# Six pairs of 1024-wide projections computed as seven block products each, ahead of the state-space branch

## The chip, the cores and the metric

One core of one Trainium2 chip runs the whole program: two transformer blocks on 1024 tokens of width 1024, in float32. The metric is the device time of one execution in microseconds (us), as the median of several runs; lower is better.

## What is computed

The change touches only the first block. With `x` of 1024 tokens by 1024 features it computes (cut to what matters):

```
xn   = rmsnorm(x, attn_norm_g)
proj = xn @ w_in                      # 38 feature tiles of 128: 0-3 pool, 4-9 / 10-15 / 16-21 q / k / v of
                                      # dilated attention, 22-33 q, k, v of stick-breaking, 34-37 state space
y_pool, y_dil, y_sb, y_s5 = the four branches of proj
for b, yb in enumerate((y_pool, y_dil, y_sb, y_s5)):
    merged += sigmoid(xn @ w_gate[b]) * (yb @ w_branch[b])   # w_gate: 4 x 8 feature tiles of 128
x = x + merged @ w_out                # then a gated FFN, then the second block
```

The second block is modulated by `cond @ w_ada`, a vector-matrix product whose 48 tiles of 512 KB are read and reduced while the first block is still running ("conditioning").

## The kernel before

**Layout and products.** Activations are kept transposed, features on partitions. A *product* (`product`, `product_steps`) is one output tile of 128 features by 1024 tokens: for each of 8 input tiles of 128 features, three float32r matmuls (high part of weight and input, then each low part with the other's high part) for each half of 512 tokens, 48 matmuls of 128x128 by 512. One input tile (6 matmuls) is a *step*. The normalised input is held as `XH[0]` (high part, `xhi`) and `XH[1]` (low part, `xlo`). A product with 4 input tiles (`w_br3`, `w_br0`, `w_glu`) has 24 matmuls.

**Weights.** `weight_plan` lists every product in the order in which TensorE takes them (`PLAN`). A ring of three buffers serves them: SyncE loads unit i+5 into `raw` (`load_weights`), ScalarE rounds unit i+2 to `whi` (`weights_hi`, L436), VectorE subtracts to `wlo` (`weights_lo`, L441). `begin_sp`, `begin_act` and `begin_dve` are called at unit i on each engine; `weights_hi` of unit j must wait until the product of unit j-3 is over, because it shares that buffer. No scheduler orders anything: each engine runs its own hand-written sequence and waits on counters.

**Order in the first block.** `input_*` normalises x and computes `w_in` tiles 34 and 35; `s5_*` is the state-space branch. Its own matmuls are small, so 13 products (`BESIDE`: `w_in` 36, 37 and eleven gates in `EARLY_S5`) are cut into steps and put between its stages by the table `SLOTS` (21 steps beside the making of `CL`, 3 and 10 beside the kernel rows, and so on). Early gates leave for DRAM (`spill`) and come back in their merge. `merge_*(3)` then multiplies gates and branch products, `pool_*`, `merge_*(0)`, `dil_*` (dilated attention, three groups g), `merge_*(1)`, `sb_*`, `merge_*(2)` follow. In a merge, turn ft computes gate ft+1 (only if it isn't early; 48 matmuls) and branch product ft (24 matmuls in merges 3 and 0). Beside merges 3, 0 and 1, conditioning (`cond_*`) takes 3 steps per turn, one before the branch product and two after: a step is one 512 KB load into a ring of three `adr` buffers on SyncE and one multiply-add into `ada` on VectorE (L1244, L1247); after 8 of them TensorE turns `ada` into 8 columns (L1271), from which VectorE makes `mod`.

**Dilated attention** starts each group with products for k and v (in group 0 also q), each copied out of PSUM by ScalarE (`K`, `Vf`, L1712), then transposes v (`turned`), and then interleaves scores, softmax and outputs of 8 blocks with the steps of the next group's q products.

**Seven products.** The two FFN up-projections already compute a pair of 1024-deep products as seven block products instead of eight (`seven_pe`, L2517). Two weight tiles by two halves of the inputs make a 2x2 block matrix, and tokens are cut in halves too; with sums of weight blocks (on GpSimd, L2480 to L2489) and of input blocks (made once), seven products of 4 input tiles by 512 tokens, 12 matmuls each, are enough, and additions on VectorE and GpSimd (`P1`, `U2`, `U3`, `P5`; tile name `prt`) make the four results.

Of the kernel before, what the change touches and what calls it, by code (L numbers as in the profile page):

```python
# [8 lines left out]
F32 = mybir.dt.float32  # L9
# [5 lines left out]
T = 1024  # L15
# [67 lines left out]
EARLY_S5 = ((3, 2), (3, 4), (3, 6), (0, 0), (0, 2), (0, 4), (0, 6), (1, 0), (1, 6), (2, 6), (3, 0))  # L83
# [4 lines left out]
EARLY = EARLY_S5 + EARLY_DIL + EARLY_SB  # L88
# [12 lines left out]
def weight_plan():  # L101
# [22 lines left out]
    tiles("w_in", range(34, 38), 8)  # L124
    tiles("w_gate", [8 * b + ft for b, ft in EARLY_S5], 8)
# [4 lines left out]
    tiles("w_in", [4, 5], 8)  # L130
    for g in range(3):
        tiles("w_in", [10 + 2 * g, 11 + 2 * g, 16 + 2 * g, 17 + 2 * g] + ([6 + 2 * g, 7 + 2 * g] if g < 2 else []), 8)
# [46 lines left out]
def used_part(i):  # L179
# [26 lines left out]
    "sums_dve": "x_add sq_add t1_sum sum1 t2_sum t_sum2",  # L206
# [160 lines left out]
def build(nc, A, out, scr, spill, bsc, hid):  # L367
    from contextlib import ExitStack
    ctx = ExitStack()
    with ctx:  # L370
# [228 lines left out]
        def input_act(act):  # L599
# [13 lines left out]
            def high(k, hf):  # L613
                act.wait_ge("xn_g", k, hf)
                hi_of(act, XH[0][:, k, half[hf]], xtmp[k % 3][:, half[hf]], "xn_hi", k, hf)
# [18 lines left out]
        def input_dve(dve):  # L634
# [6 lines left out]
            def low(k, hf):  # L641
                dve.wait_ge("xn_hi", k, hf)
                lo_of(dve, XH[1][:, k, half[hf]], xtmp[k % 3][:, half[hf]], XH[0][:, k, half[hf]], "xn_lo", k, hf)

            for hf in range(2):
                dve.wait_ge("xn_rstd", hf)
                for k in range(8):
                    if k >= 3:
                        dve.wait_ge("xn_lo", k - 3, hf)
                    dve.e.scalar_tensor_tensor(xtmp[k % 3][:, half[hf]], X[:, k, half[hf]], vec("attn_g", k), xrstd[:, half[hf]], ALU.mult, ALU.mult).then_inc(*give("xn_g", k, hf))  # L650
# [9 lines left out]
            weights_lo(dve, 2)  # L660
            for g in range(3):
# [4 lines left out]
            next(powers, None)  # L666
            begin_dve(dve, "w_in", 34)
            begin_dve(dve, "w_in", 35)
            s5_coefficients(dve)

        XNH = [(XH[0][:, k, :], XH[1][:, k, :], (("xn_lo", k, 0), ("xn_lo", k, 1))) for k in range(8)]
        XN = [(hi, lo, ready[1]) for hi, lo, ready in XNH]
# [15 lines left out]
        q1 = mem("q1", u_at - 1280, [128, 4, 16])  # L688
        q2 = mem("q2", u_at - 1024, [128, 16, 16])
# [26 lines left out]
        def s5_powers(dve):  # L716
# [47 lines left out]
            for _ in range(2):  # L764
                tt(t1, si, si, ALU.mult)
                stt(si, si, 2.0, co, ALU.mult, ALU.mult)
                ts(co, t1, -2.0, 1.0, ALU.mult, ALU.add)
            tt(nr, mag, co, ALU.mult)
# [16 lines left out]
        def s5_coefficients(dve):  # L785
# [15 lines left out]

            for _ in range(3):
# [4 lines left out]

            b3 = lambda x: x.unsqueeze(2).to_broadcast([128, 16, 16])
# [29 lines left out]

        BESIDE = [("w_in", 36), ("w_in", 37)] + [("w_gate", 8 * b + ft) for b, ft in EARLY_S5]
        BESIDE0 = PLAN.index(("w_in", 36, 0, 8))  # L840
        SLOTS = [("cl", 21), ("k", 3), ("ks", 10)]
# [3874 lines left out]
```

## Time and profile before

| | us |
|---|---|
| median of 3 runs | 3344.96 |
| lowest, highest | 3342.58, 3346.75 |
| the profiled execution, own time | 3346.08 |
| its span in the trace | 3344.40 |

TensorE is busy in 3267.9 of the 3344.4 us. The trace gives for each instruction its start, its length, the idle time before it on its engine and the instruction that ended that idle time. The length of a matmul in the trace includes its way through the array and overlaps the next one; the pace of TensorE is read from the distance of starts. Two matmuls of the same form are merged into one row ("x2").

### The profile page before, as it was taken

The numbers are of one execution on the slowest core, as the hardware profiler recorded it, in microseconds if no ns is written. First come the engines' busy times: TensorE is split into PE (matmuls) and PEld (weight loads), VectorE is DVE, ScalarE is ACT, GpSimd is POOL, SyncE is SP. The second block draws the span as 40 slices with busy tenths as digits, with TensorE's granted clock in tenths as the row PEclk, the third lists the DMA queues.
The fourth block names the chain that finished last, engine by engine and source line by source line (L and its number), as shares of the span: only waits on it lengthen the run. The fifth ranks groups of instructions, "written<-read, shape, count | busy, mean of one in ns | idle before, by whom it ended". The sixth has DMA issues, their size and how long they took to land.

```text
span 3344.4 us, 38691 instructions
## 1 busy us (share of the span) xinstructions
PE 3267.9 (98%) x15672; PEld 2676.9 (80%) x15672; DVE 1955.6 (58%) x2362; ACT 1317.5 (39%) x1888; POOL 467.6 (14%) x369
## 2 busy tenths in 40 slices
PE   8999999999999999999999999999989999999998
PEld 6888888877877778888888887777788778888886
DVE  8564462333756534677773265445476788888226
ACT  4342211444256523433331147343555554444213
POOL 0000000000000000445540020000020025554000
PEclk9999999999999999999999999999999999999999
DMA  3313242112520123233238323121204322234721
GB/s 125 78 57 132 92 162 72 46 51 68 193 70 27 62 85 131 88 112 114 101 113 334 130 85 114 62 99 44 102 1 170 114 88 109 105 114 164 304 98 51
DMA packets 116402, 356.91 MB, mean 107 GB/s; under 512 B 16232, under 2 KB 26216, under 8 KB 116208
## 3 DMA queue, kind: packets, MB, share of 16 engines
q1 hardware_dynamic: 114112, 354.10, 30.6%
q8 instruction: 124, 2.03, 0.3%
q10 hardware_dynamic: 2112, 0.33, 0.1%
q14 instruction: 54, 0.44, 0.0%
HBM read 267.63 MB, written 85.58 MB: 106 GB/s over the span
## 4 chain that ended last, share of the span: by engine, by line
PE 86%; DVE 6%; ACT 5%; issue 1%; DMA 1%; ACTq 0%; SPq 0%; DVEq 0%
PE PS L496 45%; PE PS L2517 22%; PE PS L479 8%; PE PS L1980 1%; PE PS L514 1%; PE PS L1633 1%; ACT whi L436 1%; ACT dS L1689 1%; PE PS L3961 1%; DVE wlo L441 0%; DVE FT L3834 0%; PE PS L3972 0%; PE PS L1608 0%; DVE GS L3490 0%; DVE dO L1754 0%
## 5 line engine op out<-in xcount | busy, mean ns | idle before, releaser
L441 DVE TENSOR_TENSOR wlo<-raw,whi 128x1024 fp32r<-128x1024 f32 (+3 forms) x380 | 482.5, 1270 | 389.5 <-ACT whi L436 386.7
L436 ACT CAST whi<-raw 128x1024 fp32r<-128x1024 f32 (+3 forms) x380 | 359.1, 945 | 690.2 <-PE PS L496 339.8
L496 PE MATMUL PS<-xhi,whi 128*128 128x512 f32 x1872 | 600.3, 402 | 7.3 <-DVE wlo L441 2.8
L496 PE MATMUL PS<-xlo,whi 128*128 128x512 f32 x1872 | 578.1, 390 | 0.0
L496 PE MATMUL PS<-xhi,wlo 128*128 128x512 f32 x1872 | 577.1, 389 | 0.0
L496 PEld LDWEIGHTS PS<-xhi,whi 128*128 128x128 f32 x1872 | 344.3, 188 | 91.8 <-issue 15.4
L496 PEld LDWEIGHTS PS<-xlo,whi 128*128 128x128 f32 x1872 | 351.4, 188 | 75.2
L496 PEld LDWEIGHTS PS<-xhi,wlo 128*128 128x128 f32 x1872 | 351.4, 188 | 74.8
L2517 PE MATMUL PS<-tf,whi 128*128 128x512 f32 x936 | 288.0, 389 | 0.0
L2517 PE MATMUL PS<-xhi,whi 128*128 128x512 f32 x624 | 243.5, 390 | 2.5 <-DVE xlo L2502 2.5
L2517 PE MATMUL PS<-xlo,whi 128*128 128x512 f32 x624 | 243.2, 390 | 0.0
L2517 PE MATMUL PS<-xhi,wlo 128*128 128x512 f32 x624 | 243.2, 390 | 0.0
L2517 PEld LDWEIGHTS PS<-tf,whi 128*128 128x128 f32 x936 | 175.7, 188 | 36.4
L2517 PE MATMUL PS<-tf,wlo 128*128 128x512 f32 x468 | 182.1, 389 | 0.0
L2116 POOL TENSOR_SCALAR_AFFINE_SELECT sbt<-sbt 128x128 f32<-128x128 f32 x64 | 17.8, 293 | 1072.8 <-DVE sbt L2137 1041.8
L2517 PEld LDWEIGHTS PS<-xhi,whi 128*128 128x128 f32 x624 | 117.5, 188 | 27.2 <-DVE xlo L2502 3.0
L2480 POOL TENSOR_TENSOR raw<-raw 128x512 f32<-128x512 f32 x39 | 76.0, 1948 | 438.3 <-DVE wlo L441 328.6
L2517 PEld LDWEIGHTS PS<-xlo,whi 128*128 128x128 f32 x624 | 117.6, 188 | 24.4
L2517 PEld LDWEIGHTS PS<-xhi,wlo 128*128 128x128 f32 x624 | 117.4, 188 | 24.5
L479 PE MATMUL PS<-xhi,whi 128*128 128x512 f32 x256 | 109.7, 429 | 6.3 <-DVE xlo L530 5.3
L496 PE MATMUL PS<-yhi,whi 128*128 128x512 f32 x352 | 109.1, 391 | 1.1 <-ACT gearly L888 1.1
L479 PE MATMUL PS<-slot,whi 128*128 128x512 f32 x352 | 110.1, 394 | 0.0
(613 smaller groups left out, 5482.4 us busy)
## 6 DMA issues: line engine op xcount, KB each, us to landing
raw<-in_w_up SPq DMA_DIRECT2D x88, 512.0 KB, 4.0
hid<-hs SPq DMA_DIRECT2D x88, 512.0 KB, 3.6
raw<-in_w_in SPq DMA_DIRECT2D x67, 512.0 KB, 3.5
slot<-hid SPq DMA_DIRECT2D x56, 512.0 KB, 6.8
adr<-in_w_ada SPq DMA_DIRECT2D x48, 512.0 KB, 4.8
raw<-in_w_down SPq DMA_DIRECT2D x40, 512.0 KB, 3.6
raw<-in_w_gate SPq DMA_DIRECT2D x32, 512.0 KB, 3.5
merged<-hid SPq DMA_DIRECT2D x16, 512.0 KB, 12.4
```

The source lines that it names most:

```text
L436: act.e.copy(whis[place(i)][:, ks, :], raws[i % RING][:, ks, :]).then_inc(*give("w_hi", i))
L441: dve.e.tensor_tensor(wlos[place(i)][:, ks, :], raws[i % RING][:, ks, :], whis[place(i)][:, ks, :].bitcast(F32), ALU.subtract).then_inc(*g ...
L479: ins = pe.e.matmul(ps[:, half[hf]], w[s][:, k, :], x[:, half[hf]], start=(at == 0 and n == 0), stop=(at == kt - 1 and n == 2))
L496: ins = pe.e.matmul(ps[:, h * 512:(h + 1) * 512], w[s][:, k, :], x[:, h * 512:(h + 1) * 512], start=(at == 0 and n == 0), stop=(at == kt - ...
L514: ins = pe.e.transpose(ps[:, j * 128:(j + 1) * 128], src[:, j * 128:(j + 1) * 128], ident)
L1633: ins = pe.e.matmul(ps[:, 64 * h:64 * h + 64], dP[u % 2][:, n, k, :], Vt[:, k0 // 128 + k, 64 * h:64 * h + 64], start=(k == 0), stop=(k == ...
L1689: act.e.activation(S[:, h, 256 - W:256], S[:, h, 256 - W:256], ACT.Exp, bias=st[:, h:h + 1], accum_out=O[:, 260 + h:261 + h]).then_inc(*gi ...
L1980: pe.e.matmul(ob[:, cs], sbVt[:, kb, :], sbwk[n % 4][0][:, cs], start=u["first"], stop=(kb == 0), skip_group_check=True).then_inc(*give("s ...
L2116: pool.e.affine_select(out=t[:, ds], in_=t[:, ds], pattern=[[1, 128]], compare_op=ALU.is_gt, fill=0.0, base=0, channel_multiplier=-1).then ...
L2480: pool.e.tensor_tensor(s[:, 0:4, :], b[:, 0:4, :], b[:, 4:8, :], ALU.add).then_inc(*pool.step())
L2517: ins = pe.e.matmul(ps, ws[w][:, at + k, :], xs[:, k, :], start=(k == 0 and n == 0), stop=(k == 3 and n == 2))
L3961: ins = pe.e.matmul(ps[:, sl[n]], Me[:, sl[n]], odd[:, sl[n]], start=True, stop=True)
```

## The change

1. `PASS` names six pairs: gates (3,3) and (3,7), gates (0,3) and (0,7), `w_in` 4 and 5 (q of group 0), and `w_in` 16/17, 18/19, 20/21 (v of the three groups). They are taken out of the merges and of dilated attention and computed by a new stage between `w_in` 37 and the state-space work, each pair as seven block products (`pass_pe`). Their 12 results go to DRAM (`pass_store`) and are read back where they are used.
2. The input sums `PT` are made in place in `X` by VectorE (`pass_sum`), split by `pass_hi` and `pass_lo`; one of them overwrites tiles 0 to 3, second half, of `XH`, which is saved to DRAM before (`xn_saved`) and loaded back after the last use (`xn_back`). To free that use early, the last pair computes its p5 first. The first product after the stage takes input tiles 4 to 7 first.
3. `w_in` 36 and 37 run ahead of the stage; the small operations for the state-space coefficients (`s5_powers`, `s5_coefficients`) are cut in pieces and run between VectorE's work for pairs 1 to 4. The state-space stage has 12 gates beside it (2,5 is new); its first slots are 9, 5 and 12 steps.
4. In merges 3 and 0 conditioning takes 4 + 2 steps in a turn that has a gate product and 2 + 0 in a turn that has none.
5. Group 0 of dilated attention starts with k instead of q, and all groups have no v product; q and v are loaded from DRAM.

```diff
+PASS = ((("w_gate", 27), ("w_gate", 31)), (("w_gate", 3), ("w_gate", 7)), (("w_in", 4), ("w_in", 5)),
+        (("w_in", 16), ("w_in", 17)), (("w_in", 18), ("w_in", 19)), (("w_in", 20), ("w_in", 21)))
...
+        def pass_pe(pe):
...
+                if p == NPASS - 1:
+                    part(s12, 0, PTF[1], "p5", ("sv_p5", 0, p), "sv_5", 0, p)
+                part(a, 0, PX11, "p1", ("sv_p1", 0, p), "sv_1", 0, p)
+                part(a, 4, PX21, "p2", ("sv_c11", 0, p), "prod", a)
+                pe.wait_ge("t_lo", 0, 4)
+                part(b, 4, PTF[4], "p4", ("sv_c21", 0, p), "prod", b)
+                pe.wait_ge("t_lo", 0, 1)
+                if p < NPASS - 1:
+                    part(s12, 0, PTF[1], "p5", ("sv_p5", 0, p), "sv_5", 0, p)
+                pe.wait_ge("t_lo", 0, 2)
+                part(s12, 4, PTF[2], "p6", ("sv_u2", 0, p), "prod", s12)
+                part(s34, 0, PTF[3], "p7", ("sv_u3", 0, p), "sv_7", 0, p)
+                part(s34, 4, PX22, "p3", ("sv_c12", 0, p), "prod", s34)
...
+        def pass_act(act):
+            for p in range(NPASS):
+                begin_act(act, *PASS[p][0])
+                if p == 0:
+                    pass_hi(act, 1)
+                    pass_hi(act, 2)
+                else:
+                    act.wait_ge("sv_c12", 0, p - 1)
...
+        def pass_dve(dve, others):
...
+                begin_dve(dve, *PASS[p][1])
+                if p:
+                    next(beside, None)
+                begin_dve(dve, "pass_s12", p)
+                dve.wait_ge("prod", i + 2)
...
+        def pass_sp(sp):
...
+                begin_sp(sp, "pass_s34", p)
+            sp.wait_ge("sv_5", 0, NPASS - 1)
+            for m in range(2):
+                sp.e.dma_start(PTF[1][m].bitcast(F32), BACKUP[m]).then_inc(*land("xn_back", m))
...
-        SLOTS = [("cl", 21), ("k", 3), ("ks", 10)]
+        SLOTS = [("cl", 9), ("k", 5), ("ks", 12)]
...
+        def beside_steps(b, ft):
+
+            if b not in (3, 0):
+                return 1, 2
+            return (2, 0) if (b, ft + 1) in EARLY or ft == 7 else (4, 2)
...
-                for n, ring in enumerate((side_ring, o_ring)):
-                    product(pe, ring, "w_in", 16 + 2 * g + n, XN, ("dil_v", g, n))
                 turned(g, 0)
```

Three places show what the change moves. The first is VectorE in merge 3, turns 0 to 3 (`merged` is the multiply with the branch product, `ada` a conditioning step, `mod` the wait for TensorE's 8 columns). Before:

```order
L1348 TENSOR_TENSOR merged_79<-PS,gearly_135 128x1024 [waits gate,prod]
L1244 TENSOR_SCALAR ada_141<-adr_138,cond_52 128x1024 [waits cond,adr0]
...
L1348 TENSOR_TENSOR merged_79<-PS,sgl_136 128x1024 [waits gate,prod]
...
L1348 TENSOR_TENSOR merged_79<-PS,sgl_137 128x1024 [waits gate_in0,prod]
L1247 SCALAR_TENSOR_TENSOR ada_141<-adr_138,cond_52,ada_141 128x1024 [waits ada,adr0]
L1247 SCALAR_TENSOR_TENSOR ada_141<-adr_139,cond_52,ada_141 128x1024 [waits ada,adr1]
L441 TENSOR_TENSOR wlo_62<-raw_56,whi_59 128x512 [waits w_hi]
L1348 TENSOR_TENSOR merged_79<-PS,sgl_136 128x1024 [waits gate,prod]
L1258 TENSOR_TENSOR mod_51<-PS,V_49 128x8 [waits pe_sums]
```

Now:

```order
L1603 TENSOR_TENSOR merged_79<-PS,gearly_135 128x1024 [waits gate,prod]
L1493 SCALAR_TENSOR_TENSOR ada_154<-adr_151,cond_52,ada_154 128x1024 [waits ada,adr0]
L1493 SCALAR_TENSOR_TENSOR ada_154<-adr_152,cond_52,ada_154 128x1024 [waits ada,adr1]
L1493 SCALAR_TENSOR_TENSOR ada_154<-adr_153,cond_52,ada_154 128x1024 [waits ada,adr2]
L1493 SCALAR_TENSOR_TENSOR ada_154<-adr_151,cond_52,ada_154 128x1024 [waits ada,adr0]
L446 TENSOR_TENSOR wlo_63<-raw_57,whi_60 128x512 [waits w_hi]
L1603 TENSOR_TENSOR merged_79<-PS,sgl_136 128x1024 [waits gate,prod]
L1493 SCALAR_TENSOR_TENSOR ada_154<-adr_152,cond_52,ada_154 128x1024 [waits ada,adr1]
L446 TENSOR_TENSOR wlo_64<-raw_58,whi_61 128x1024 [waits w_hi]
L1603 TENSOR_TENSOR merged_79<-PS,sgl_137 128x1024 [waits gate_in0,prod]
L1504 TENSOR_TENSOR mod_51<-PS,V_49 128x8 [waits pe_sums]
```

The eighth `ada` step stood after the third `merged`, with the fourth `merged` and its turn behind it before TensorE's columns; now it stands after the second `merged`, and TensorE's columns come right ahead of the fourth branch product.

The second place is ScalarE at the start of group 1 of dilated attention (`K` and `Vf` are the copies of k and v out of PSUM). Before:

```order
L436 CAST whi_61<-raw_58 128x1024 [waits w_raw2]
L1712 COPY K_119_167<-PS 128x256x4 [waits prod]
L436 CAST whi_59<-raw_56 128x1024 [waits w_raw0]
L1712 COPY Vf_168<-PS 128x256x4 [waits prod]
L436 CAST whi_60<-raw_57 128x1024 [waits w_raw1]
L1712 COPY Vf_168<-PS 128x256x4 [waits prod]
L1689 ACTIVATE dS_173,dO_179<-dS_173,dstat_178 128x128 [waits dil_st00,dil_dve]
```

Now:

```order
L441 CAST whi_60<-raw_57 128x1024 [waits w_raw1]
L1978 COPY K_132_180<-PS 128x256x4 [waits prod]
L441 CAST whi_61<-raw_58 128x1024 [waits w_raw2]
L1957 ACTIVATE dS_186,dO_192<-dS_186,dstat_191 128x128 [waits dil_st00,dil_dve]
```

Between the last copy of k and the first exponential of the scores two v products with their copies are gone.

The third place is SyncE at the last pair of the new stage (`put` is a result on its way out, `xhi` and `xlo` from `spill` are the input tiles that come back). Nothing like it was there before. Now:

```order
L1050 DMA spill<-put_148 128x1024
L434 DMA raw_58<-in_w_gate 128x1024 [waits w_lo]
L1063 DMA xhi_75<-spill 128x4x512 [waits seven_pe]
L1063 DMA xlo_76<-spill 128x4x512
L1050 DMA spill<-put_149 128x1024 [waits seven_dve]
```

The two loads that bring the input tiles back stand behind a weight load with a wait of its own.

## Rows read from the trace of the kernel before

**Rows 1.** The page: busy time, share of the span, instructions of TensorE.
```profile
PE 3267.9 (98%) x15672; PEld 2676.9 (80%) x15672; DVE 1955.6 (58%) x2362; ACT 1317.5 (39%) x1888; POOL 467.6 (14%) x369
```

**Rows 2.** Waits of TensorE, 50 to 290 us: total, times, longest.
```profile
PE PS L940 <- DVE CL L1105: 1.5, 2, 1.3
PE PS L514 <- ACT work L1041: 1.4, 1, 1.4
PE PS L496 <- DVE wlo L441: 1.3, 1, 1.3
```

**Rows 3.** Timeline of TensorE, two FFN pairs: start, length (us), operation, idle before.
```profile
1484.63 0.61 PE L2517 MATMUL PS<-tf,whi 128*128 128x512 f32 x2
...
1503.67 0.61 PE L2517 MATMUL PS<-tf,whi 128*128 128x512 f32 x2
```

**Rows 4.** Timeline of VectorE, 47 to 62 us.
```profile
51.65 3.60 DVE L700 TENSOR_SCALAR w<-w 128x16 f32<-128x16 f32 x1
...
61.53 1.22 DVE L441 TENSOR_TENSOR wlo<-raw,whi 128x1024 fp32r<-128x1024 f32 x1
```

**Rows 5.** Timeline of GpSimd, 0 to 110 us.
```profile
51.69 3.53 POOL L925 MEMSET Mk<- 128x4096 f32 x1 [51.17 <-DMA bsc<-brow]
```

**Rows 6.** Timeline of TensorE around the start of `w_in` 37.
```profile
61.01 0.61 PE L496 MATMUL PS<-xhi,wlo 128*128 128x512 f32 x2
62.89 0.70 PE L496 MATMUL PS<-xhi,whi 128*128 128x512 f32 x2 [1.27 <-DVE wlo L441]
```

**Rows 7.** The FFN's input sums: min/median/max ns, starts; and TensorE's wait for them.
```profile
L2498 ACT CAST tf<-merged x4: 1901/1906/1912, 1356.9 to 2707.3; 128x2048 fp32r<-128x2048 f32 x4
...
L2502 DVE TENSOR_TENSOR tf<-merged,tf x4: 2275/2284/3376, 1362.5 to 2709.2; 128x2048 fp32r<-128x2048 f32 x4
...
PE PS L2517 <- DVE xlo L2502: 2.5, 1, 2.5
```

**Rows 8.** Timelines of ScalarE, VectorE and GpSimd in the same FFN pairs.
```profile
1484.88 1.06 ACT L436 CAST whi<-raw 128x1024 fp32r<-128x1024 f32 x1 [1.17 <-PE PS L2517]
...
1498.43 0.69 DVE L2579 TENSOR_TENSOR fsg<-PS,prt 128x512 f32<-128x512 f32 x1 [1.30 <-PE PS L2517]
1499.15 2.21 DVE L2738 TENSOR_TENSOR fsg<-fsg,rstd 128x1024 f32<-128x1024 f32 x1
...
1498.98 1.30 POOL L2489 TENSOR_TENSOR raw<-raw,raw 128x512 f32<-128x512 f32 x1
```

**Rows 9.** Timeline of VectorE: first and last of six operations for half of `CL`.
```profile
73.65 1.35 DVE L704 TENSOR_TENSOR CL<-PR,BC 128x1152 f32<-128x1152 f32 x1
...
80.61 1.36 DVE L1105 SCALAR_TENSOR_TENSOR CL<-CL,cltmp 128x1152 f32<-128x1152 f32 x1
```

**Rows 10.** DMA, 0 to 20 us: rate in 40 slices of 0.5 us; one issue's size and landing.
```profile
GB/s 0 0 0 47 185 366 336 135 160 279 287 283 324 287 320 320 332 369 410 434 434 410 401 410 406 401 402 406 402 381 389 381 385 389 422 410 406 420 415 382
...
x<-in_xT SPq DMA_DIRECT2D x16, 256.0 KB, 7.0
```

**Rows 11.** Copies of k (min/median/max ns), and TensorE where group 0's transposes start.
```profile
L1712 ACT COPY K<-PS x6: 1014/1995/2017, 552.8 to 758.6; 128x1024 f32<-128x1024 f32 x6
...
585.26 1.03 PE L514 MATMUL PS<-ident,Vf 128*128 128x128 f32 x8
586.23 0.71 PE L1608 MATMUL PS<-K,Qs 64*128 64x128 f32 x8
```

**Rows 12.** VectorE in merge 0, a conditioning step's length, and the landing of its loads.
```profile
467.50 1.22 DVE L1350 TENSOR_TENSOR sg<-PS,sg 128x1024 f32<-128x1024 f32 x1 [2.22 <-PE PS L496]
...
469.90 2.67 DVE L1247 SCALAR_TENSOR_TENSOR ada<-adr,cond,ada 128x1024 f32<-128x1024 f32 x2
...
L1247 DVE SCALAR_TENSOR_TENSOR ada<-adr,cond,ada x28: 1273/1283/1289, 306.4 to 504.6; 128x1024 f32<-128x1024 f32 x28
...
DMA to landing us min/median/max: 3.7/4.8/7.0
```

**Rows 13.** Merge 3: length, then busy us and instructions of PE, PEld, DVE, ACT, POOL, clock, DMA share, GB/s.
```profile
290.00:376.50 86.50, 86.50 (x391) 71.91 (x390) 42.69 (x41) 16.06 (x20) 0.00 (x0) 1.00 0.51 172
```

More of the change, by code:

```diff
@@ L863, in stream @@
                 for p, (name, ft) in enumerate(BESIDE):
-                    done = ("s5_u", ft - 34) if name == "w_in" else ("gate", ft // 8, ft % 8)
-                    yield from product_steps(pe, [0, 1] if p % 2 == 0 else [1, 0], name, ft, XN, done)
+                    order = (4, 5, 6, 7, 0, 1, 2, 3) if p == 0 else None
+                    yield from product_steps(pe, [0, 1] if p % 2 == 0 else [1, 0], name, ft, XN, ("gate", ft // 8, ft % 8), order=order)
             steps = stream()
@@ L909, in s5_sp @@
             begin_sp(sp, "w_in", 35)
+            sp.wait_ge("xn_lo", 3, 1)
+            for m in range(2):
+                sp.e.dma_start(BACKUP[m], PTF[1][m].bitcast(F32)).then_inc(*land("xn_saved", m))
+            begin_sp(sp, "w_in", 36)
+            begin_sp(sp, "w_in", 37)
+            pass_sp(sp)
             beside_sp(sp, "cl")
@@ L928, in s5_pe @@
             rows_ring = [2, 3]
+            for n in range(2):
+                product(pe, [n], "w_in", 36 + n, XN0, ("s5_u", 2 + n))
+            pass_pe(pe)
             beside = beside_pe(pe)
@@ L1341, in merge_dve @@
                     branch(dve)
-                next(beside, None)
+                for _ in range(beside_steps(b, ft)[0]):
+                    next(beside, None)
                 i = begin_dve(dve, f"w_br{b}", ft)
@@ L1355, in merge_dve @@
                     dve.e.tensor_tensor(merged[:, ft, :], merged[:, ft, :], g, ALU.add).then_inc(*give("merged", b, ft))
-                next(beside, None)
-                next(beside, None)
+                for _ in range(beside_steps(b, ft)[1]):
+                    next(beside, None)
                 if done:
@@ L1381, in merge_sp @@
                     branch(sp)
-                next(beside, None)
+                for _ in range(beside_steps(b, ft)[0]):
+                    next(beside, None)
                 begin_sp(sp, f"w_br{b}", ft)
-                next(beside, None)
-                next(beside, None)
+                for _ in range(beside_steps(b, ft)[1]):
+                    next(beside, None)
             for _ in beside:
```

279 lines of the change are left out of this document (231 added, 48 removed).

## The prediction, made before the changed kernel ran

> **What bounds the kernel now.** I read the page's busy times first: TensorE is busy for 3267.9 of 3344.4 us [rows 1], so only fewer TensorE cycles or fewer TensorE waits can save time, and a new wait of TensorE costs its full length. Next the waits of TensorE where the new stage goes: they are small and single, 1.5 us for `CL`, 1.4 us for `work`, 1.3 us for a `wlo` [rows 2]. Then the pace, from the one place where seven-product pairs already run: the same part of two consecutive FFN pairs starts at 1484.63 and 1503.67 us, so 84 matmuls take 19.04 us, 0.2267 us each, with no idle time noted on any row between [rows 3]. The reader should see that a pair, once running, costs exactly its matmuls: VectorE, ScalarE and GpSimd keep up. What has to be found is what happens at the stage's two ends, and in the three stages that lose products.
>
> **The matmuls.** A pair as two products has 2 x 48 = 96, as seven block products 7 x 12 = 84. Six pairs save 72 x 0.2267 = **16.3 us**. The compiled sequences agree: TensorE has 72 matmuls fewer and no other form changes its count. The new stage adds per pair 5 additions on VectorE, 6 on GpSimd, 2 copies on ScalarE and two more weight splits. FFN pairs carry all of these and more, so in the steady part I cost them at nothing; the cover is VectorE's slack, about 11 of 19 us per pair (4 splits and 5 additions are some 8 us). The small coefficient operations that are put into pairs 1 to 4 take at most about 8 us in one piece, so they fit; if they didn't, TensorE would wait at the next pair's p1.
>
> **What is removed before the stage.** `w_in` 37 starts at 62.89 where its predecessor's pace ends at 61.01 + 2 x 0.2267 = 61.46: 1.43 us [rows 6]. The cause is on VectorE: the `wlo` runs at 61.53, behind a chain of 16-element operations one of which takes 3.60 us instead of 0.17 [rows 4], exactly while GpSimd's memset of `Mk` runs [rows 5]. Both move away; the split then stands behind two sums of 2.3 us and is over near 56 us. Gain **1.4 us**. The other new work here (four sums, two splits by ScalarE and VectorE, the 2 MB save to DRAM) has until p1, 4 or p5 need it, from 72 us on, and by the same lengths it is ready by 69 us.
>
> **The first pair.** One input sum overwrites tiles that `w_in` 37 reads, so its chain starts only when that product ends: copy of U 1.0, weight rounding 1.05, `pass_hi` 1.9, `pass_lo` 2.28, `pass_hi` 1.9, `pass_lo` 2.28 [rows 7, 8] with 0.3 for the first signal: 10.7 us. TensorE has p1, p2, p4, p5 to do, 4 x 2.72 = 10.9. It just fits; the FFN's similar start costs 2.5 us [rows 7]. I take 0.3, between 0 and 2.5.
>
> **The last pair.** Its p5 comes first. p5's weights lie in the buffer that the previous pair's p3 is still reading, so their rounding can't start before that ends: 0.25 us after TensorE's pace passes on (1484.63 and 1484.88) [rows 3, 8], 1.06 of rounding, then VectorE 1.15. But at a pair's boundary GpSimd still has its two weight differences: at 1498.98 for 1.30 us, 0.75 to 2.05 us after the boundary at 1498.23 (19.04 us before p1 of the next), and the VectorE operation with two inputs from SBUF that meets it takes 2.21 instead of 1.22 us [rows 8]. So the split starts at 2.05 and TensorE at **3.3 us**; without that meeting 2.6, with a full one 4. In all other pairs this chain has 8.2 us of cover. The Trainium skill (SBUF — State Buffer, Who interferes with whom) says that a VectorE instruction with two SBUF inputs contends with a GpSimd instruction that reads SBUF and that the loser fully blocks; the trace agrees (2.21 against 1.22 us), and with it the sum has 3.3, without it 2.6.
>
> **The way back.** The tiles that were saved must be back 4 steps after the stage, 24 x 0.2267 = 5.4 us after its end. Although p5 is over early, SyncE reaches these loads only behind a weight load that waits for a split behind p6, 13.6 us into the last pair; with 0.3 signal, 1.05 and 1.2 for the split the issue is at 16.3, and 2.6 MB at the 400 GB/s of the start [rows 10] take 6.5 us. A start-up of 2.4 us comes on top: the fastest 512 KB landing took 3.7 us [rows 12], 1.3 of it data at that rate. That lands at 25.2, where 19.0 + 5.4 = 24.4 is needed. I take **0.8 us**; with the transfers already flowing it is 0, at 250 GB/s it would be 4.8. The page DMA: Bandwidth & Descriptors (Specifications) of the Trainium skill gives about 358 GB/s as the limit of HBM per core; by it the wait would be 1.6 us, but the trace's slices of 400 to 434 speak against it.
>
> **The state-space stage.** Its first slot shrinks from 21 steps to 9, 54 x 0.2267 = 12.2 us. VectorE needs 0.3 + 1.05 + 1.2 for a weight split and 5 x 1.39 + 1.36 = 8.3 for the first half of `CL` [rows 9]: 10.9. So that wait of TensorE (1.5 us) goes too, by a margin of 1.3. The `work` wait (1.4 us) hung on the DMA of `Mk`, which SyncE issued 9 us late, behind an early gate's store; with this gate's store now before it and 2 steps more beside it, it goes. Gain **2.9 us**, with 0 as the other end.
>
> **Merges 3 and 0.** Both lose two gate products, so three turns in a row have only 24 matmuls, 5.44 us. TensorE's 8 columns for the first `ada` now stand ahead of the fourth branch product, 2 x 5.44 = 10.9 us after the first ended (P), behind VectorE's five `ada` steps, one split and one or two `merged`. In merge 0: `merged` 2.7 after P (467.50 to 469.90, with 0.3 from the product's end) [rows 12], `ada` at 1.3 each to 6.6; the next needs a load that could be issued only when a buffer was free, at 4.0, and lands 4.8 later: 8.8, done 10.1; split 0.7, `merged` 2.4, `ada` 1.3: 14.4 with the signal. TensorE waits 3.4; with the shortest landing (3.7) 2.3, with the longest (7.0) 5.6 [rows 12]. In merge 3 each of the two `merged` is one operation of 1.2 us instead of two: the same chain ends 2.3 us earlier, and TensorE waits 1.1 (0 to 3.3). Sum **4.5 us** (2.3 to 8.9).
>
> **Dilated attention.** k's last copy was covered by two v products. Now only 8 transposes, 0.97 us [rows 11], stand between the product and the first scores. The copy starts 0.3 after, takes 1.0 in group 0 and 2.0 in groups 1 and 2 [rows 11], 0.1 signal: waits of 0.4, 1.4 and 1.4, **3.2 us**. The v and q loads (2 MB for group 0) have 21.8 us of cover.
>
> **Sum.** -16.3 - 1.4 - 2.9 + 0.3 + 3.3 + 0.8 + 4.5 + 3.2 = -8.5 us. The profiled execution's own time is 3346.08 (span 3344.40, the rest lies around it and doesn't change); it would become 3337.6. It lies 1.1 above the median of 3344.96, and the median, which I predict, becomes **3336.5**.
>
> **Rivals.** (A) *All new waits hide.* For it: the tables look made to fit, and each margin above is near 1 us. Against it: last pair and copies of k rest on lengths that don't vary. Only those two at their low ends (2.6, 3.0) and 1 us in the merges: 3344.96 - 20.6 + 6.6 = 3331. (B) *The ends and merges run at their high ends*: first pair 2.5, last 4, way back 4.8, merges 8.9, k 3.2 = 23.4, less 16.3, 1.4 and half of 2.9: 3349 if all come at once; with half of the excess 3343. For it: the same loads took up to 7.0 us when several were queued [rows 12]. (C) *Slower: DMA bounds the short turns.* Turns 1 to 3 of each of the two merges move about 9 pieces of 512 KB, 4.7 MB in 16.3 us, 289 GB/s, and VectorE, which waits for the loads in order, also makes the weights. At 170 GB/s they would take 27.7 us, 11.4 more twice: 3336.5 + 22.8 = 3359. It decides from about 200 GB/s down (23.5 us, 7 more each: 3350). Against it: before, three loads, a gate and weights fell into single short turns, and TensorE was busy in all 86.5 us of merge 3 [rows 13]. (D) *The stage doesn't do what it says*: the pairs run at the pace of the other engines, since results are written in other strides here (two of ScalarE's three-way copies take 2.0 instead of 1.0 us [rows 11]). At 1 us per pair 3342.
>
> **Chances.** Forecast (3334 to 3339) 0.46, of which 0.43 is below 3338.3; A 0.17; B and D together 0.30, of which 0.05 is still faster and 0.02 slower; C 0.04; the remaining 0.03 for faults that I don't see, half of it slower. 0.2% is 6.7 us, about what a measurement of this kernel tells from no change: faster is below 3338.3, slower above 3351.7. Faster 0.43 + 0.17 + 0.05 = 0.65, slower 0.02 + 0.04 + 0.01 = 0.07, same 0.28. The range takes A and half of B: 3329 to 3343.5.
>
> **What would show it.** TensorE with 72 fewer matmuls; in the last pair a wait for `wlo` near 3.3 us ahead of p5; a wait for `ada` before the 8 columns, near 1 in merge 3 and 3 in merge 0; three waits for `K`, 0.4, 1.4, 1.4; no wait for `CL` or `work`; the pairs at 19.04 us. The prediction is wrong if pairs are longer than 19.1 us, if the waits for `ada` are absent or above 6 us, or if `xn_back` holds TensorE for more than 4 us.

## The result, and the profile after

The changed kernel takes **3366.4 us** (median of four runs, 3364.0 to 3368.2), the kernel before 3344.9: a ratio of 1.0064 with a 95% interval of 1.0047 to 1.0082. It is slower by 21.5 us where I had forecast 3336.5. One of the eleven runs of experiment 7 below took 4260 us at a mean granted clock of 0.72 and, being in another state of the chip, is left out of the range given there. The profiled execution has a span of 3362.3 us, 17.9 more than before. Its TensorE line, in the columns of [rows 1]:

```profile
PE 3262.0 (97%) x15600; PEld 2669.1 (79%) x15600; DVE 2018.7 (60%) x2412; ACT 1332.9 (40%) x1908; POOL 518.0 (15%) x405
```

The 72 matmuls are gone, but TensorE's busy time fell by 5.9 us, not by 16.3. So what is left was slower, by some 10 us in all, and on top TensorE stood still for longer: the rest of the span grew from 76.5 to 100.3 us. Where, four stretches of 50 us show; the columns are the stretch, its length, TensorE's busy time and instructions, the clock granted to TensorE in tenths of full speed, the DMA share and GB/s. The kernel before:

```profile
150.00:200.00 50.00, 49.91 (x361) 1.00 0.18 58
200.00:250.00 50.00, 48.89 (x285) 1.00 0.19 59
450.00:500.00 50.00, 50.00 (x231) 1.00 0.59 201
550.00:600.00 50.00, 49.04 (x240) 1.00 0.13 43
```

The changed kernel (the work in a stretch is not the same, the busy share and the clock are what to compare):

```profile
150.00:200.00 50.00, 43.17 (x182) 0.96 0.51 177
200.00:250.00 50.00, 46.14 (x298) 0.94 0.39 89
450.00:500.00 50.00, 49.21 (x226) 0.97 0.57 192
550.00:600.00 50.00, 39.51 (x159) 0.86 0.56 184
```

In each of the four, idle time has come in and the granted clock has fallen. From 50 to 150 us, where `w_in` 36 and 37 and four of the six pairs run, TensorE waits for nothing and is busy in every microsecond: the pairs themselves keep the pace of [rows 3]. The waits (total, times, longest) from 150 to 210 us, from 210 to 300, from 300 to 500 and, the last two lines, in merge 0:

```profile
PE PS L501 <- DMA xlo<-spill: 3.7, 1, 3.7
PE PS L939 <- DVE wlo L446: 3.1, 1, 3.1
PE PS L1195 <- ACT WT L1297: 3.9, 1, 3.9
PE PS L1517 <- DVE ada L1493: 2.1, 1, 2.1
PE PS L1517 <- DVE ada L1493: 9.4, 1, 9.4
PE PS L501 <- DVE wlo L446: 1.1, 1, 1.1
```

These are, in order, the way back of the saved tiles, the last pair's p5, one in the state-space stage that I had not foreseen, the conditioning in merges 3 and 0, and a weight split in merge 0. The waits of [rows 2] for `CL`, `work` and `wlo` are gone.

**What follows a wait.** TensorE's timeline at the last pair's p5 (start, length, operation, idle before; lines of single matmuls):

```profile
165.54 0.39 PE L939 MATMUL PS<-xhi,wlo 128*128 128x512 f32 x1
169.02 0.77 PE L939 MATMUL PS<-xhi,whi 128*128 128x512 f32 x1 [3.09 <-DVE wlo L446]
169.59 0.63 PE L939 MATMUL PS<-xlo,whi 128*128 128x512 f32 x1
...
172.49 0.39 PE L939 MATMUL PS<-xhi,wlo 128*128 128x512 f32 x1
```

```profile
165.00:169.00 4.00, 0.93 (x5) 1.00 0.06 11
169.00:173.00 4.00, 3.98 (x11) 0.58 0.78 251
173.00:177.00 4.00, 4.00 (x19) 1.00 0.00 0
```

For 3.4 us behind the wait the matmuls last 0.63 instead of 0.39 us and start every 0.43 instead of every 0.2267 us; the granted clock of the 4 us is 0.58, of the next 4 us 1.00. So for these eight matmuls TensorE ran at the lower of its two levels, 1.2 instead of 2.4 GHz, and lost 8 x 0.2 = 1.6 us beyond the wait. The Trainium skill (TensorE: Matmul & The Clock Gate, Part 1) says that the array's clock goes down to 1.2 GHz when the engine has been idle and comes back with work; the trace agrees. My sum had no term for it. Each wait of 3 to 4 us cost about half as much again. Behind the 9.4 us in merge 0 the clock is seen to fall while TensorE still waits:

```profile
578.60:582.90 4.30, 0.00 (x0) 0.50 0.56 151
582.90:592.20 9.30, 9.26 (x30) 0.50 0.79 277
```

TensorE had the lower level for some 14 us (0.86 over 50 us: 0.14 x 50 / 0.5), but 4.3 of them lie inside the wait and cost nothing more; the 9.3 us of columns and matmuls behind it lost about half, some 4.6 us. In all, TensorE's busy time fell by 5.9 us in place of 16.3, so the lower clock cost some 10 us, about half of the loss. The mean granted clock of the span agrees: 0.996 before, 0.993 now, 0.003 x 3350 = 10 us.

This price stood in the trace of the kernel before, behind the very wait that the prediction quotes in [rows 7]: seven matmuls in 3 us, 0.43 us each.

```profile
2728.78 0.80 PE L2517 MATMUL PS<-xhi,whi 128*128 128x512 f32 x1 [2.53 <-DVE xlo L2502]
```

```profile
2728.78:2731.78 3.00, 3.00 (x7) 0.50 0.13 52
```

**Merge 0.** VectorE's timeline, from the end of the pool branch to the eighth sum:

```profile
558.08 1.23 DVE L535 TENSOR_TENSOR ylo<-pool,yhi 128x1024 fp32r<-128x1024 f32 x1 [6.74 <-ACT yhi L532]
563.15 0.76 DVE L1490 TENSOR_SCALAR ada<-adr,cond 128x1024 f32<-128x1024 f32 x1 [3.85 <-DMA adr<-in_w_ada]
564.43 2.67 DVE L1493 SCALAR_TENSOR_TENSOR ada<-adr,cond,ada 128x1024 f32<-128x1024 f32 x2 [0.52 <-DMA adr<-in_w_ada]
567.02 0.68 DVE L446 TENSOR_TENSOR wlo<-raw,whi 128x512 fp32r<-128x512 f32 x1
567.62 1.22 DVE L1605 TENSOR_TENSOR sg<-PS,sg 128x1024 f32<-128x1024 f32 x1
...
573.77 1.28 DVE L1493 SCALAR_TENSOR_TENSOR ada<-adr,cond,ada 128x1024 f32<-128x1024 f32 x1 [1.08 <-DMA adr<-in_w_ada]
577.32 1.28 DVE L1493 SCALAR_TENSOR_TENSOR ada<-adr,cond,ada 128x1024 f32<-128x1024 f32 x1 [2.27 <-DMA adr<-in_w_ada]
...
581.52 1.28 DVE L1493 SCALAR_TENSOR_TENSOR ada<-adr,cond,ada 128x1024 f32<-128x1024 f32 x1
```

The loads of the conditioning lie in the pool branch's tiles, so SyncE issues the first at 559.33 us, when the last `ylo` is done, and the first sum starts at 563.15. TensorE comes to the columns behind its third branch product, at 573.6 (582.95 less the wait of 9.37). From the first load's issue to the eighth sum it is 23.5 us; TensorE asks for it after 14.3. On the way VectorE waited three more times for a load, 3.9 us in all. The kernel before had the same start, seen in its trace (SyncE's first two loads, and the first sum):

```profile
443.73 0.80 SPq L1224 DMA_DIRECT2D adr<-in_w_ada  x2
```

```profile
448.15 0.75 DVE L1244 TENSOR_SCALAR ada<-adr,cond 128x1024 f32<-128x1024 f32 x1
```

### The profile page after: what moved, and what is told of

It reads as the page before. It is cut to its first block, busy times and chain, and to the rows that moved or that the text cites. A ratio compares the mean times of both kernels' runs of the same rounds, so it can differ in the third digit from the quotient of the medians.

```text
span 3362.3 us, 38774 instructions
## 1 busy us (share of the span) xinstructions
PE 3262.0 (97%) x15600; PEld 2669.1 (79%) x15600; DVE 2018.7 (60%) x2412; ACT 1332.9 (40%) x1908; POOL 518.0 (15%) x405
## 4 chain that ended last, share of the span: by engine, by line
PE 82%; DVE 8%; ACT 6%; DMA 2%; issue 2%; SPq 0%; ACTq 0%; DVEq 0%
PE PS L501 39%; PE PS L2779 21%; PE PS L484 8%; PE PS L939 3%; PE PS L2242 1%; DVE wlo L446 1%; ACT whi L441 1%; DMA adr<-in_w_ada 1%; PE PS L1905 1%; PE PS L519 1%; ACT dS L1957 1%; PE PS L4223 1%; DVE FT L4096 0%; PE PS L4234 0%; PE PS L1880 0%
## 5 line engine op out<-in xcount | busy, mean ns | idle before, releaser
L441 ACT CAST whi<-raw 128x1024 fp32r<-128x1024 f32 (+3 forms) x392 | 369.7, 944 | 778.2 <-PE PS L501 360.9
L446 DVE TENSOR_TENSOR wlo<-raw,whi 128x1024 fp32r<-128x1024 f32 (+3 forms) x392 | 496.3, 1266 | 299.2 <-ACT whi L441 296.2
L501 PE MATMUL PS<-xhi,whi 128*128 128x512 f32 x1680 | 542.0, 404 | 8.5 <-DMA xlo<-spill 3.7
L501 PE MATMUL PS<-xlo,whi 128*128 128x512 f32 x1680 | 520.6, 391 | 0.0
L501 PE MATMUL PS<-xhi,wlo 128*128 128x512 f32 x1680 | 519.9, 391 | 0.0
L501 PEld LDWEIGHTS PS<-xhi,whi 128*128 128x128 f32 x1680 | 309.3, 189 | 86.0 <-issue 14.1
L501 PEld LDWEIGHTS PS<-xhi,wlo 128*128 128x128 f32 x1680 | 316.4, 188 | 67.8
L501 PEld LDWEIGHTS PS<-xlo,whi 128*128 128x128 f32 x1680 | 316.3, 188 | 67.8
L2779 PE MATMUL PS<-xhi,whi 128*128 128x512 f32 x624 | 243.6, 390 | 2.6 <-DVE xlo L2764 2.6
L2779 PE MATMUL PS<-xlo,whi 128*128 128x512 f32 x624 | 243.4, 390 | 0.0
L2779 PE MATMUL PS<-xhi,wlo 128*128 128x512 f32 x624 | 243.2, 390 | 0.0
L2378 POOL TENSOR_SCALAR_AFFINE_SELECT sbt<-sbt 128x128 f32<-128x128 f32 x64 | 17.9, 295 | 951.2 <-DVE sbt L2399 920.2
L2779 PEld LDWEIGHTS PS<-xhi,whi 128*128 128x128 f32 x624 | 117.5, 188 | 27.5 <-DVE xlo L2764 3.0
L2779 PEld LDWEIGHTS PS<-xhi,wlo 128*128 128x128 f32 x624 | 117.5, 188 | 24.5
L2779 PEld LDWEIGHTS PS<-xlo,whi 128*128 128x128 f32 x624 | 117.6, 188 | 24.4
L484 PE MATMUL PS<-xhi,whi 128*128 128x512 f32 x256 | 109.3, 427 | 5.9 <-DVE xlo L535 4.8
```

The lines of the kernel that those rows point to most:

```text
L441: act.e.copy(whis[place(i)][:, ks, :], raws[i % RING][:, ks, :]).then_inc(*give("w_hi", i))
L446: dve.e.tensor_tensor(wlos[place(i)][:, ks, :], raws[i % RING][:, ks, :], whis[place(i)][:, ks, :].bitcast(F32), ALU.subtract).then_inc(*g ...
L484: ins = pe.e.matmul(ps[:, half[hf]], w[s][:, k, :], x[:, half[hf]], start=(at == 0 and n == 0), stop=(at == kt - 1 and n == 2))
L501: ins = pe.e.matmul(ps[:, h * 512:(h + 1) * 512], w[s][:, k, :], x[:, h * 512:(h + 1) * 512], start=(at == 0 and n == 0), stop=(at == kt - ...
L2779: ins = pe.e.matmul(ps, ws[w][:, at + k, :], xs[:, k, :], start=(k == 0 and n == 0), stop=(k == 3 and n == 2))
```

## The experiments

All are timed against the kernel before in the same session; "the changed kernel" has 3366.4 us.

**1. Undo the steps by length.**

```diff
         def beside_steps(b, ft):
-            if b not in (3, 0):
-                return 1, 2
-            return (2, 0) if (b, ft + 1) in EARLY or ft == 7 else (4, 2)
+            return 1, 2
```

> The changed kernel with one part undone: conditioning again takes one step ahead of every branch product and two behind it, in every merge turn, long or short. My theory is that in merge 0 the changed kernel asks for the eighth conditioning sum after three branch products (16.3 us) while the sum's loads only start with the end of the pool branch; the even steps ask for it one branch product (5.44 us) later, but DVE then has three conditioning steps (about 4.4 us) beside 3.7 us of its own work in a turn of 5.44 us. So in merge 3 the 2.1 us wait and the slow matmuls behind it (about 2 us) go; in merge 0 the wait of 9.4 us shrinks to 4 to 6 us, with a shorter stretch at the lower clock. Time 3348 to 3356, 10 to 18 us under the changed kernel's 3366.4. Rival, that short turns starve in any arrangement (DVE or the loads bound each of them): waits for wlo take the place of the wait for ada, and the time stays at 3362 to 3372. Second rival, that the conditioning's steps are innocent and the loss sits in the state-space stage: within 2 us of 3366.

Measured: 3363.6 us (3357.2 to 3366.5), ratio 1.0051 (1.0038 to 1.0063). TensorE's waits for `ada`, and merge 0's stretch:

```profile
PE PS L1517 <- DVE ada L1493: 6.0, 3, 5.1
```

```profile
550.00:600.00 50.00, 44.94 (x184) 0.90 0.57 199
```

The waits shrank as expected (merge 3 to 0.6, merge 0 to 5.1 us), the median by only 2.8 us, outside my 3348 to 3356. Its interval overlaps that of the changed kernel (1.0047 to 1.0082), so the 2.8 us are not clear of the noise. Waits and clock in merge 0 account for some 10 us in this profile, and it has two stretches of 6.8 us at the lower clock in and behind the dilated attention, where the changed kernel's has one of 3.4. So the steps by length are a part of the waits, 5.5 us of them; merge 0 is short of cover with even steps too.

**2. Take the columns later.** TensorE's columns of the first sum (and VectorE's reading of them) in merges 3 and 0 move two turns back, behind the second gate product:

```diff
-                if i % 8 == 7:
+                if (i % 8 == 7 and (i > 7 or j0 == 4)) or (i == 9 and j0 < 4):
+                    n = 7 if i == 9 else i
```

> The changed kernel, with the columns of each merge's first conditioning sum on TensorE taken two turns later (behind the second gate product of merges 3 and 0); DVE's sums and the loads stay where they are. If the loss in the merges is only that TensorE asks too early, the waits of 2.1 us (merge 3) and 9.4 us (merge 0) and the slow matmuls behind both (about 2 and 7 us) go: 3344 to 3348. If DVE itself is late in merge 0 (its wlo for the second gate product stands behind the eighth sum, at 582.7 us, where TensorE would want it at 579), a wait for wlo of 3 to 4 us with a short stretch at the lower clock takes the place of the larger one: 3349 to 3353. If the short turns are bound by the loads all through, nothing is won: above 3360.

Measured: 3358.1 us (3351.6 to 3360.3), ratio 1.0035 (1.0023 to 1.0047). The waits for `ada` are gone in both merges; in merge 0 another takes their place, and VectorE's timeline shows what makes it:

```profile
PE PS L501 <- DVE wlo L446: 6.1, 2, 4.8
```

```profile
572.31 1.28 DVE L1493 SCALAR_TENSOR_TENSOR ada<-adr,cond,ada 128x1024 f32<-128x1024 f32 x1 [1.66 <-DMA adr<-in_w_ada]
573.51 0.68 DVE L446 TENSOR_TENSOR wlo<-raw,whi 128x512 fp32r<-128x512 f32 x1
```

The split of the next weights stands on VectorE behind a sum that waits for its load. This was the second case of the expectation, 5 us dearer than its upper end (3349 to 3353 expected). Asking later saves 8 us, but what is missing is TensorE work beside the conditioning.

**3. The loads back, earlier.** The last pair's loop issues them right behind its first weight load:

```diff
                 begin_sp(sp, *PASS[p][0])
+                if p == NPASS - 1:
+                    sp.wait_ge("sv_5", 0, NPASS - 1)
+                    for m in range(2):
+                        sp.e.dma_start(PTF[1][m].bitcast(F32), BACKUP[m])...
                 begin_sp(sp, *PASS[p][1])
```

> The changed kernel with the two loads that bring back the first half of the input's high and low parts issued as soon as the last pair's block product p5 has been read (about 172.3 us), ahead of two weight loads and two stores, instead of behind them at 188.1 and 189.3 us. Theory: TensorE's wait for them (3.7 us at 195.2) and the slow matmuls behind it (about 1.7 us) go, 5.4 us in all, about 3361. Rival: the first gate product then waits for its weights instead, or the clock falls anyway: 3364 to 3367.

Measured: 3364.1 us (3358.0 to 3366.3), ratio 1.0052 (1.0039 to 1.0065). The wait of 3.7 us is gone from the trace; 2.3 of the expected 5.4 us are seen, with intervals wider than that: the trace shows that the wait went, the medians don't show what it was worth. This trace has the lower clock at places where the changed kernel's doesn't, in and behind the dilated attention and in merge 2.

**4. And p5 in its usual place in the last pair**, on top of edit 3.

```diff
-                if p == NPASS - 1:
-                    part(s12, 0, PTF[1], "p5", ...)
...
-                if p < NPASS - 1:
-                    part(s12, 0, PTF[1], "p5", ...)
+                part(s12, 0, PTF[1], "p5", ...)
```

> As the run before, and the last pair computes p5 in its usual place as the fourth block product instead of the first. TensorE's wait for wlo at 165.8 us (3.1 us) and the slow matmuls behind it (1.7 us) go as well; the loads back are issued near 176.5 us and should still land by 187, ahead of 195: 3356 to 3358, 8 to 11 us under the changed kernel. Rival: the wait for wlo only moves to the fourth block product, or the loads back land late: 3360 to 3364.

Measured: 3358.1 us (3351.0 to 3361.2), ratio 1.0036 (1.0023 to 1.0048), 8.3 us under the changed kernel. No wait is left there, and in the stretch of the last pair the clock stays up:

```profile
150.00:200.00 50.00, 49.57 (x248) 1.00 0.54 190
```

Between this run and the one before lies 5.9 us for a wait of 3.1 us and its slow matmuls (4.8 expected).

**5. One part of the change alone, on the kernel before:** only the steps by length (`beside_steps` as in the change).

> The kernel before, with one part of the change alone: the conditioning's steps by the length of each merge turn in merges 3 and 0 (six in a turn with a gate product, two in one without). Its merge 0 still has four gate products, so the columns of the first sum stand behind two branch products and one gate product counted from the end of the pool branch (21.8 us) instead of behind four and one (32.7 us). The eighth sum took 24 us from the pool's end in the changed kernel, so a wait of 0 to 3 us and at most one short stretch at the lower clock: 3344 to 3350. Rival, that the steps themselves cause the changed kernel's waits whatever the gate products do: a wait near 9 us, above 3355. If it is the missing gate products alone, within 2 us of 3345.

Measured: 3355.3 us (3353.1 to 3357.6), ratio 1.0032 (1.0020 to 1.0045): 10.8 us slower than before, outside my 3344 to 3350. Merge 3 has no wait for the columns. In merge 0, behind the pool branch, TensorE waits twice:

```profile
PE PS L1271 <- DVE ada L1247: 4.4, 1, 4.4
PE PS L496 <- DVE wlo L441: 1.7, 1, 1.7
```

With six steps in a long turn the columns stand two branch products sooner than before, and TensorE waits even with all gate products in place. The first load was issued at 441.23 us, TensorE asked at 461.5, 20.3 us later, and the eighth sum was ready after 24.6. The time is that of the expectation's rival (above 3355), the wait half of the 9 us that the rival had. So in merge 0 each half of the change hurts: the missing gate products (experiment 1 keeps 5.1 us of wait) and the uneven steps (6.1 us here).

**6. The wait in the state-space stage.** ScalarE's largest wait before the two copies to `WT`, in the changed kernel, and what SyncE's queue does then:

```profile
ACT gearly L1119 <- DMA spill<-gearly: 13.8, 1, 13.8
```

```profile
230.97 6.82 SPq L1136 DMA_DIRECT2D Mk<-Ks  x4
237.83 2.48 SPq L1133 DMA_DIRECT2D spill<-gearly  x1
```

ScalarE may overwrite the gate's tile only when its store has landed, and the store is issued behind four loads into `Mk` that hold the queue for 6.8 us. The edit puts the store ahead of them:

```diff
         def beside_sp(sp, slot):
-            for kind, p in slot_events(slot, 0, 0):
+            for kind, p in slot_events(slot, 0, -2):
```

> The changed kernel, with SP storing the second early gate of the state-space stage ahead of the four loads into Mk instead of behind them. In the changed kernel ScalarE waits 13.8 us for that store, because its issue stands behind 6.8 us of Mk issues, and the two copies to WT that TensorE needs stand behind ScalarE's wait. Theory: the 3.9 us wait for WT at 243 us and the slow matmuls behind it (about 1.7 us) go: 3360 to 3362. Rival: the Mk loads now come later and TensorE waits for them or for Ug instead: 3364 to 3368.

Measured: 3362.6 us (3358.0 to 3368.0), ratio 1.0053 (1.0039 to 1.0066). The wait for `WT` is gone, 0.5 us for `work` is left, and ScalarE's wait for the store is 5.2 us. 3.8 of the expected 5.6 us are seen in the medians, and the intervals overlap, so only the trace shows this wait's cause.

**7. Other gate products.** The passes compute gates 1 and 7 of merge 2 instead of 3 and 7 of merge 0; merge 0 has its gate products and even steps back. The count of matmuls stays 15600.

```diff
-PASS = ((("w_gate", 27), ("w_gate", 31)), (("w_gate", 3), ("w_gate", 7)), ...
+PASS = ((("w_gate", 27), ("w_gate", 31)), (("w_gate", 17), ("w_gate", 23)), ...
...
-            if b not in (3, 0):
+            if b != 3:
                 return 1, 2
```

> The changed kernel, with the second pair of the passes computing gate products 1 and 7 of merge 2 instead of 3 and 7 of merge 0, and merge 0's conditioning back at one step ahead and two behind; merge 2 has no conditioning beside it. The number of matmuls is the same. Theory (the loss in merge 0 is DVE's sums and their loads having too little TensorE work beside them from the end of the pool branch on): the waits of 1.1 and 9.4 us and the slow matmuls (about 7 us) go, merge 2 stays without new waits over 2 us: 3346 to 3351. Rival: merge 2 with gate products nowhere starves instead (DVE has 3.7 us of its own work and 1.2 us of low parts in a branch product of 5.44 us, and six gates come back from memory): waits of 5 us and more in merge 2, 3355 to 3366.

Measured: 3346.3 us (3343.0 to 3349.7), ratio 1.0005 (0.9996 to 1.0014): 20.1 us under the changed kernel, as expected. Merge 0 first, then the waits of merge 2:

```profile
550.00:600.00 50.00, 50.00 (x226) 1.00 0.57 194
600.00:650.00 50.00, 50.00 (x231) 1.00 0.49 170
```

```profile
PE PS L501 <- DVE wlo L446: 2.9, 2, 2.5
```

Merge 0's 10.5 us of waits are gone, and merge 2, which has no conditioning beside it, pays nothing for its two products: in the changed kernel, which still computes them there, it waits 3.1 us (0.4, 2.6 and 0.2). This is the largest part of the loss, and it lies in what stands beside merge 0's conditioning. The edit undoes both halves of the change there at once. By itself the return to even steps was worth 2.8 us (experiment 1), which leaves some 17 us for the gate products; against the 10.8 us that uneven steps cost with all gate products in place (experiment 5) it would be some 9. The halves don't simply add, and the gate products' return under uneven steps was not run on this kernel.

**8. All mends together:** 3, 4, 6 and 7, and experiment 2 for merge 3 alone.

> All the mends together: the loads back ahead and p5 in its usual place in the last pair, the second early gate's store ahead of the Mk loads, merge 3's first columns two turns later, and the gates of merge 2 in place of merge 0's with even steps there. Each removes a wait and the slow matmuls behind it: 5.4 + 4.8 + 5.6 + 4 + 17.5 us, so near 3329 if they add up and the product's saving of 16.3 us is real, range 3323 to 3337, faster than both kernels. If the clock falls somewhere else in its place (each fall costs 1.7 us), or merge 2 starves, 3337 to 3345.

Measured: **3329.1 us** (3326.1 to 3330.6), ratio 0.9953 (0.9941 to 0.9966). TensorE's line of this kernel:

```profile
PE 3254.3 (98%) x15600; PEld 2665.3 (80%) x15600; DVE 2018.6 (61%) x2412; ACT 1330.8 (40%) x1908; POOL 523.9 (16%) x405
```

15.4 us under the kernel before: the saving of the block products is there once nothing gives it back.

**9. The same without any step by length:** `beside_steps` returns 1, 2 everywhere, and merge 3's columns stay where they were.

> The kernel with all the mends (3329.1 us), but merge 3's conditioning also back at one step ahead of every branch product and two behind it, with its columns where they first were; no step goes by the length of a turn any more. It asks what the second half of the change is worth by itself. The changed kernel with even steps everywhere waited 0.6 us for ada in merge 3 with the clock at 1.00, so I expect no loss: 3327 to 3331. Rival, that merge 3, with two gate products where it had four, needs the uneven steps: a wait for wlo or ada of 2 us and more and a stretch at the lower clock, 3333 to 3338.

Measured: **3328.4 us** (3326.5 to 3330.9), ratio 0.9944 (0.9930 to 0.9957). The uneven steps are not needed anywhere; merge 3 waits 0.9 us.

**10 and 11. What a wait costs.** On the kernel of experiment 8, a wait that nothing needs, behind every second branch product of merges 0, 1 and 2 (in 11 on `merged` in place of `br`):

```diff
+                if b != 3 and ft % 2:
+                    pe.wait_ge("br", b, ft)
```

> A measurement of what a wait costs TensorE, on the kernel with all the mends (3329.1 us). In merges 0, 1 and 2, TensorE waits behind every second branch product (12 times) until DVE has multiplied that product with its gate, a wait that nothing in the computation needs. DVE's multiplication takes 1.22 us and starts about 0.2 us behind the product, so 12 waits of about 1.4 us, 17 us. If a wait of that length costs only itself, the time is 3345 to 3348 and the granted clock in the merges stays at 1.00. If each wait is followed by a stretch at the lower clock (3.4 us in which matmuls take 0.43 instead of 0.227 us, so 1.6 us lost), 3364 to 3368.

> As the run before, but TensorE waits for DVE's addition to merged too, so 12 waits of about 2.7 us, 32 us. If a wait costs only itself, 3360 to 3363. If each is followed by one stretch at the lower clock, 20 us more, 3379 to 3384. The changed kernel's own waits of 3 to 4 us were each followed by one such stretch and one of 1.1 us by none, so I expect p1_br at the price of its waits alone and this run near the upper figure, or between the two if only some waits are followed by one.

Measured: 3379.0 us (3377.8 to 3379.2), ratio 1.0101 (1.0086 to 1.0116), and 3398.2 us (3397.1 to 3400.6), ratio 1.0162 (1.0145 to 1.0179). Both miss, since many waits were longer than planned, 4 to 9 us. In merges 0 and 1 VectorE was behind with its conditioning when the product ended (at the 6.8 us wait in merge 1, three sums of 4.05 us stood ahead of the multiplication). In merge 2, where there is none, the multiplication stood behind the next weights' split, which itself waited 2.8 us for ScalarE's rounding. Two lines of TensorE's timeline in 10, both in merge 2, and the 8 us behind each of them:

```profile
1257.68 0.73 PE L501 MATMUL PS<-yhi,whi 128*128 128x512 f32 x2 [4.17 <-DVE sg L1611]
1271.79 0.73 PE L501 MATMUL PS<-yhi,whi 128*128 128x512 f32 x2 [1.32 <-DVE sg L1611]
```

```profile
1257.68:1265.68 8.00, 8.00 (x28) 0.79 0.60 194
1271.79:1279.79 8.00, 8.00 (x35) 1.00 0.44 140
```

Behind 4.17 us 28 matmuls fit into 8 us, behind 1.32 us 35. In 11, behind 5.31 and 2.58 us:

```profile
1273.89:1281.89 8.00, 8.00 (x28) 0.78 0.50 150
1289.29:1297.29 8.00, 8.00 (x35) 1.00 0.41 131
```

In the merges of the two kernels, all 13 waits of 4.1 us and more ahead of a product were followed by the lower clock, and none of the seven of 1.3 to 2.85 us (two of them ahead of smaller matmuls). Elsewhere shorter waits were followed too: of the waits of 2.4 to 2.65 us for `wlo` in merge 2, which nine of the traces have, five were (experiments 2, 3, 7, 8 and 9), and the 2.5 us in the kernel before. Ahead of the conditioning's columns (eight columns of one element, 16 records in the trace, on which TensorE spends 1.7 us where it did not wait) it was otherwise: two waits of 1.3 and 1.5 us and two of 2.6 and 2.7 us were followed by it, as was every such wait of 1.8 us and more in the other runs. In 10 the span is 47.2 us longer than in 8. TensorE's busy time, 3266.7 against 3254.3 us with the same matmuls, takes 12.4 of them, and the waits the other 34.8; the mean clock, 0.991 against 0.995, stands for 0.004 x 3376 = 14 us, but part of the slow time lies inside waits.

## Why the prediction was wrong

- **The matmuls and the pairs: right.** 72 fewer, the pairs at the pace foreseen, no wait in the first pair (0.3 predicted), the waits for `wlo` of `w_in` 37, `CL` and `work` gone. Experiments 8 and 9 show that this saving is real.
- **The last pair: the wait right, its price not.** 3.3 us predicted, TensorE resumed 3.25 us late, through the same meeting of VectorE and GpSimd (the split took 1.78 us). But the first eight matmuls then cost 1.6 us more.
- **The way back: mis-sized.** 0.8 us predicted (0 to 4.8), 3.7 measured, and slow matmuls behind it. The loads were issued at 188.05 and 189.26 us, and the second took 9.8 us to land: 11.0 us from the first issue, where I had 8.9 from rate and start-up. The issue came 22.3 us into the last pair, 1 us later than my 16.3 and the 4.9 us of wait and slow matmuls at the pair's start.
- **The state-space stage: a step missing.** I wrote that a gate's store was now ahead of the `Mk` loads, and took the gain of 2.9 us. The gain came, but the next gate's store now stood right behind those loads, and 3.9 us of TensorE's wait for `WT` came with it. I had followed the two waits that existed, not the queue of every store that the shorter slot moved.
- **Merge 3:** 1.1 us predicted, 2.1 measured, within its bounds.
- **Merge 0: the step that failed.** I let VectorE begin `merged` 0.3 us behind the end of the first branch product (P, 561.3 us) with three sums already done. P is worked back from the wait at 567.85: less 1.11 and one product of 24 x 0.2267. But the loads for those sums could only be issued when the pool branch had freed their tiles, at 559.33 us, the three sums ended at 567.1, and `merged` at 570.1, 8.8 us after P instead of 2.7. From there my chain is right within 1 us (12.7 us to the eighth sum, 11.7 predicted). The 6 us went through to TensorE: 9.4 + 1.1 instead of 3.4 us, with some 4.6 us of the lower clock on top.
- **Dilated attention:** 3.2 us predicted for the copies of k, 2.6 measured in three waits (0.3, 1.1, 1.1).
- **The clock: a term that was missing.** All waits together were 25.9 us new (3.1 + 3.7 + 3.9 + 2.1 + 10.5 + 2.6) against 12.1 in my sum, and the clock added some 10 us. In the profile's own books the sum's -8.5 became +17.9, 26.4 us off: 10.4 in busy time (5.9 saved instead of 16.3) and 16.0 in idle time (23.8 more instead of 12.1 - 1.4 - 2.9 = 7.8). Two waits outside the list grew as well, that for `sblo` at the start of stick-breaking from 1.3 to 2.3 us, with 3.4 us at the lower clock behind it, and merge 2's for `wlo` from 1.5 to 3.1; why, no run asked. Without the clock the changed kernel would have stood near 3356, still slower than before.

The rivals: (C) named the right place, the short turns of the merges, and the right sign, but its mechanism was the rate of the loads, with some 200 GB/s as the point from which it would decide. From the first load's issue to the eighth sum, 559 to 583 us, the DMA engines moved 243 GB/s; what mattered first was when the first load could be issued. That the landings (5.1 us in the median) have no part in it is not shown, since 3.9 us of VectorE's chain are waits for later loads. I gave it 0.04. (A), (B) and (D) did not happen. My falsifier for the merges (an `ada` wait above 6 us) is what was seen.

What stays open: why the same waits, those of 1.1 to 1.2 us in the dilated attention and of 2.4 to 2.65 us in merge 2, are followed by the lower clock in one trace and not in another. The mean granted clock differs between runs of one kernel as their times do (experiment 4: 0.994 at 3351 us, 0.991 at 3361), and stretches of this kind hid part of the gains of experiments 1 and 3. The remaining 2.9 us of waits in merge 2 I left as they are.

## What to carry to other kernels

When work is taken from TensorE, ask in which turns it was the cover of something else: two gate products taken from merge 2, which has no conditioning, added no wait there; taken from merge 0, together with the uneven steps, they cost 20 us more. For a chain of sums, begin the count where its first load can be issued, and follow every store and load that a shorter slot moves past a long issue in a queue. Look in the trace at the matmuls behind each wait of TensorE, and price a wait of 3 us or more at its length plus 1.6 us; one of 2.4 to 2.65 us cost that in about half of the traces here. Do not put tiny matmuls right behind a wait.

## What the runs showed of the hardware

- Waits of 3 to 4 us between products brought TensorE to its lower level for 3.4 us (matmuls every 0.43 us) nearly every time; one of 3.3 us, in experiment 7, did not. In merge 0 it was there for some 14 us, of which 4.3 were the end of the 9.4 us wait.
- Waits of 2.4 to 2.65 us ahead of full products in merge 2 were followed by the lower level in five of nine traces.
- Waits of 1.3 and 1.5 us ahead of the one-column matmuls (experiment 10) were followed by the lower level; waits of 1.3 us ahead of full products never were in the merges.
- Four loads that spread 16 partitions of `Ks` over `Mk` hold SyncE's queue for 6.8 us in issuing, and the 512 KB store behind them landed 7.0 us after its issue, against 2.7 us in the median.
